# A layer step with a routed mixture of experts on one core: the first expert pair's tokens gathered by a product, late loads untied from the gather, the combine moved between two gates, the last down product in column halves

## The reference, cut to what matters

```python
def hier_moe(h, rg_w, rg_b, re_w, re_b, w_gate, w_up, w_down):
    ...
    lg = tf @ rg_w.astype(jnp.float32) + rg_b.astype(jnp.float32)
    grp = jnp.argmax(lg, axis=-1)
    ...
    top_v, top_i = lax.top_k(le, TOP_K_INNER)
    ...
    acc = jnp.zeros_like(t)
    for e in range(N_EXPERTS):
        hid = jax.nn.silu(t @ w_gate[e].astype(t.dtype)) * (t @ w_up[e].astype(t.dtype))
        acc = acc + combine[:, e:e + 1] * (hid @ w_down[e].astype(t.dtype))
    return acc.reshape(shp)
```

## Time and profile before

| | |
|---|---|
| median of 3 runs | 820.41 us (819.87 to 823.77) |
| the profiled execution's own time | 821.48 us |
| its span in the trace | 819.8 us |
| PE busy | 772.7 us (94%) |
| DVE, ACT, POOL busy | 270.4, 158.6, 139.1 us |
| mean rate of the DMA engines | 304 GB/s over the span |

### The profile page before, as it was taken

One profiled execution on the slowest core, in us unless ns is written; L12 is line 12 of the kernel. 1 busy time (PEld: TensorE's weight loads), 2 busy tenths in 40 slices (PEclk: granted clock), 3 DMA queues, 4 the chain that ended last, 5 costly groups with the idle time before them and its releaser, 6 DMA issues.

```text
span 819.8 us, 8712 instructions
## 1 busy us (share of the span) xinstructions
PE 772.7 (94%) x3488; PEld 372.7 (45%) x3488; DVE 270.4 (33%) x614; ACT 158.6 (19%) x313; POOL 139.1 (17%) x167
## 2 busy tenths in 40 slices
PE   4999999989999999889999999999998999899996
PEld 3777677758743334544333333333333333333332
DVE  2059999995355632521111101110110111011001
ACT  3211121234541101300211111111111111101114
POOL 2069899702002000010000000000000000000000
PEclk9999999999999999989999999999999999999999
DMA  9894200041508189989999999999999999999981
GB/s 275 301 350 166 103 20 0 2 110 41 167 26 265 57 276 348 419 320 427 426 426 426 427 429 424 427 429 425 426 426 428 426 426 427 427 428 426 429 335 65
DMA packets 51256, 249.58 MB, mean 304 GB/s; under 512 B 6966, under 2 KB 24406, under 8 KB 38655
## 3 DMA queue, kind: packets, MB, share of 16 engines
q1 hardware_dynamic: 45540, 243.54, 74.1%
q10 hardware_dynamic: 3147, 2.67, 1.1%
q0 software_dynamic: 2528, 2.79, 1.1%
HBM read 246.87 MB, written 8.61 MB: 312 GB/s over the span
## 4 chain that ended last, share of the span: by engine, by line
PE 71%; DVE 4%; issue 3%; ACT 2%; DMA 0%; DVEq 0%; ACTq 0%; POOLq 0%
PE bank L1177 27%; PE bank L1200 14%; PE bank L1051 9%; PE bank L1218 8%; PE bank L1160 2%; PE bank L1189 1%; PE bank L1024 1%; PE bank L1015 1%; DVE bank L1571 1%; PE bank L788 1%; PE bank L1178 1%; PE bank L1040 1%; PE bank L885 1%; DVE bank L1600 1%; DVE region_a L1570 1%
## 5 line engine op out<-in xcount | busy, mean ns | idle before, releaser
L788 PE MATMUL bank<-region_a,ring 128*128 128x320 f32 x576 | 158.7, 437 | 0.5 <-DVE region_a L1570 0.5
L1178 PE MATMUL bank<-ring,zz 128*64 128x512 f32 x304 | 135.3, 601 | 0.0
L788 PEld LDWEIGHTS bank<-region_a,ring 128*128 128x128 f32 x576 | 109.8, 192 | 46.5 <-issue 2.2
L1177 PE MATMUL bank<-ring,zz 128*64 128x512 f32 x272 | 122.9, 608 | 8.6 <-issue 8.0
L1570 DVE TENSOR_TENSOR region_a<-region_a,bank 64x512 f32<-64x512 f32 (+1 forms) x33 | 22.5, 680 | 328.6 <-ACT region_a L1497 328.4
L1571 DVE SCALAR_TENSOR_TENSOR bank<-region_a,par,bank 128x256 f32<-128x256 f32 x232 | 91.2, 483 | 0.0
L744 POOL DMA_INDIRECT region_a<-hn_scratch,region_a x16 | 15.9, 995 | 379.1 <-PE bank L1160 362.6
L1218 PE MATMUL bank<-zz,masks 128*128 128x512 f32 (+1 forms) x192 | 75.3, 609 | 2.1 <-ACT zz L1503 2.1
L1177 PEld LDWEIGHTS bank<-ring,zz 128*64 128x64 f32 x272 | 37.1, 140 | 83.7 <-issue 82.9
L1051 PE MATMUL bank<-ring,x_v_y 128*128 128x512 f32 (+1 forms) x192 | 74.1, 606 | 0.8 <-DVE x_v_y L1570 0.8
L1503 ACT ACTIVATE zz<-bank 64x512 f32<-64x512 f32 x64 | 37.8, 591 | 169.5 <-PE bank L1200 169.1
(11 more groups left out here) (310 smaller groups left out, 806.2 us busy)
## 6 DMA issues: line engine op xcount, KB each, us to landing
ring<-in_expert_w_up SPq DMA_DIRECT2D x19, 2048.0 KB, 33.7
ring<-in_expert_w_down SPq DMA_DIRECT2D x18, 2048.0 KB, 38.0
ring<-in_expert_w_gate SPq DMA_DIRECT2D x16, 2048.0 KB, 35.6
ring<-in_w_in SPq DMA_DIRECT2D x9, 2048.0 KB, 20.0
x_v_y<-in_expert_w_down SPq DMA_DIRECT2D x7, 2048.0 KB, 28.0
x_v_y<-in_expert_w_gate SPq DMA_DIRECT2D x5, 2048.0 KB, 42.5
ring<-in_w_out SPq DMA_DIRECT2D x4, 2048.0 KB, 9.1
xcx<-in_expert_w_gate SPq DMA_DIRECT2D x4, 2048.0 KB, 35.8
```

What stands on the lines that cost most here:

```text
L788: ins = pe.matmul(pt[0:m, 0:T], w[:, k, :], ht[:, k, :], start=k == 0, stop=k == KD - 1)
L1177: pe.matmul(to[0:CAP, :], x[:, k, :], wg[:, FE * k:FE * k + FE], **st)
L1178: ins = pe.matmul(to[CAP:P, :], x[:, k, :], wu[:, FE * k:FE * k + FE], **st)
```

## The change

It has four parts.

1. **First pair by a product.** Pair 0 isn't gathered. DVE builds `first`, a one-hot selection of tokens by slots for experts 0 and 1, scaled by 1/rms, and PE multiplies the raw rows in `xt` with it: `first_tokens(h)`, 12 products of 128 x 128, for each half. They stand around the `slots` product, and the `residual` products are spread: tile 1's first half goes ahead of `rank`, tile 2 behind it, tile 1's second half last. POOL gathers pairs 1 to 15.
2. **Late loads.** Load 8 waits for the router's last logits alone, load 9 for `hn_out`, load 10 still for `kept`.
3. **Combine between gates.** combine(i-2) stands between gate_up(2i) and gate_up(2i+1).
4. **The end.** The last down product is made in two column halves, in two banks; ACT copies the first half while PE makes the second; the last combine goes by column halves, with the 64-token tile last; the final norm follows that order, and the sample output's second half is stored from ACT's queue.

```diff
@@ SP
             sp_.wait_ge(filled, J[("lg2",)] + 1)
+            load_expert(n_slot - 3)
             sp_.wait_ge(S("hn_out"), 48)
-            load_expert(n_slot - 3)
-            sp_.wait_ge(S("gath"), 16)
             load_expert(n_slot - 2)
             sp_.wait_ge(S("kept"), 1)
             load_expert(n_slot - 1)
@@ PE
             residual(0)
+            residual(1, [0])
             pe.wait_ge(S("chosen"), 1)
...
             counts(ones, 2, 3, start=False, stop=True).then_inc(filled, 1)
+            residual(2)
...
+            def first_tokens(h):
+                to = job_bank("tokens", (0, h))
+                for k in range(4):
+                    for r, (t0, n) in enumerate(TILES):
+                        if h == 0 and k == 0:
+                            pe.wait_ge(S("first"), r + 1)
+                        ins = pe.matmul(to[:, P * k:P * k + P], xt[0:n, r, 4 * h + k:D:KD], first[0:n, r, :],
+                                        start=r == 0, stop=r == 2)
+                ins.then_inc(S("xg_T"), 1)
+                return ins
...
+            first_tokens(0)
             pe.wait_ge(S("osel"), 1)
-            slot_values(take(pe, "slots")).then_inc(filled, 1)
-            residual(1)
-            residual(2).then_inc(S("kept"), 1)
+            slot_values(take(pe, "slots"), osel).then_inc(filled, 1)
+            first_tokens(1)
+            residual(1, [1]).then_inc(S("kept"), 1)
...
+            def down_half(to, x, wd, q):
+                for k in range(4):
+                    for h in range(2):
+                        c0 = D * k + 512 * q + 256 * h
+                        ins = pe.matmul(to[CAP * h:CAP * h + CAP, 0:256], x[:, k, :], wd[:, c0:c0 + 256],
+                                        start=k == 0, stop=k == 3)
+                return ins
...
             for i in range(NE // 2):
                 for e in (2 * i, 2 * i + 1):
+                    if i >= 2 and e % 2:
+                        combine(i - 2)
                     gate, up = expert_landed(pe, 0, e), expert_landed(pe, 1, e)
...
                 if more:
-                    pe.wait_ge(S("gath"), 16 * (i + 2))
-                    tokens_T(i + 1, 0)
-                if i >= 2:
-                    combine(i - 2)
-                if more:
-                    tokens_T(i + 1, 1)
+                    pe.wait_ge(S("gath"), 16 * (i + 1))
+                    for h in range(2):
+                        tokens_T(i + 1, h)
...
             expert_down(NE - 2)
-            expert_down(NE - 1)
+            w_down = expert_landed(pe, 2, NE - 1)
+            down_half(job_free(pe, "down", NE - 1), hidt[:, :, own_half[1]], w_down, 0).then_inc(S("dn_half"), 1)
+            pe.wait_ge(S("hidt"), NE // 2)
+            down_half(job_bank("hidden", NE // 2 - 1), hidt[:, :, own_half[1]], w_down, 1).then_inc(S("dn_done"), 1)
...
+            pe.wait_ge(S("yo_half"), 1)
+            for r in range(2):
+                to_tile(back[1], yo_of, r, 0, end=True).then_inc(S("summed"), 1)
             pe.wait_ge(S("yo"), NE)
-            to_tokens(back[1], yo_of, end=True)
+            for r in range(2):
+                to_tile(back[1], yo_of, r, 1, end=True).then_inc(S("summed"), 1)
+            to_tile(back[1], yo_of, 2, 0, end=True)
+            to_tile(back[1], yo_of, 2, 1, end=True).then_inc(S("summed"), 1)
@@ DVE
+            link(dve.tensor_scalar(first_off, aa[:, :, 0:2], -BIG, BIG, ALU.mult, ALU.add))
...
             pt = got(dve, "rank")
-            link(tt_(tee, ee, bc(r3(pt[:, 0:3 * NE]).unsqueeze(1), [P, 2, 3, NE]), ALU.mult))
+            link(tt_(first_at, r3(pt[:, 0:3 * NE])[:, :, 0:2], first_off, ALU.add))
+            for r, (t0, n) in enumerate(TILES):
+                for j in range(2):
+                    ins = dve.tensor_scalar(first[0:n, r, CAP * j:CAP * j + CAP], slotno[0:n, :],
+                                            first_at[0:n, r, j:j + 1], rst[0:n, 3 + r:4 + r],
+                                            ALU.is_equal, ALU.mult)
+                ins.then_inc(S("first"), 1)
+            tt_(tee, ee, bc(r3(pt[:, 0:3 * NE]).unsqueeze(1), [P, 2, 3, NE]), ALU.mult).then_inc(S("tee"), 1)
+            dve.tensor_copy(cnt, pt[:, 3 * NE:4 * NE]).then_inc(free["dve"], 1)
```

More of the change, by code:

```diff
@@ L145, in bank_table @@
     until.update({name: len(JOBS) for name in OUT_JOBS})
-    banks, prev, last, held, own = [], [], {}, {}, {}
+    banks, prev, last, held, own = [], [], {}, {}, {("rank",): 2, ("slots",): 2}
     b = -1
@@ L328, in build @@
         val = moe(2 * 3 * 2 * NE).rearrange("p (o u c e) -> p o u c e", o=2, u=3, c=2)
-        osel = zf[:, 0:2 * 3 * CAP].rearrange("p (o u s) -> p o u s", o=2, u=3)
+        osel, osel_more = (zf[:, D * b:D * b + 2 * 3 * CAP].rearrange("p (o u s) -> p o u s", o=2, u=3) for b in (1, 0))
+        first = r3(zf[:, 2048:2048 + 3 * P])
+        first_off, first_at = (r3(zf[:, 2048 + 3 * P + 6 * b:2048 + 3 * P + 6 * b + 6]) for b in range(2))
         slotno = moe(CAP)
@@ L740, in carry_wait @@
                 pool.tensor_tensor(wait_word[:, w:w + 1], halfrow, halfrow, ALU.add)
-            for i in range(NE // 2):
-                wait(pool, S("xg_T"), 2 * i)
+            for i in range(1, NE // 2):
+                if i > 1:
+                    pool.wait_ge(S("xg_T"), 2 * i)
                 pool.indirect_dma_start(gat, None, hn_dram[:, :],
@@ L1110, in _, with residual @@
             logits(take(pe, "lg2"), 2).then_inc(filled, 1)
-            def residual(r):
+            def residual(r, halves=range(2)):
                 n = TILES[r][1]
                 pe.wait_ge(S("x2"), r + 1)
-                for q in range(2):
+                for q in halves:
                     dst = acc[2 * r + q][:, :] if r < 2 else acc[4][TS * q:TS * q + TS, :]
@@ L1136, in _, with slot_values @@
             counts(ones, 2, 3, start=False, stop=True).then_inc(filled, 1)
-            def slot_values(pt):
+            residual(2)
+            def slot_values(pt, osel):
                 for n_, (r, w) in enumerate([(r, w) for r in range(3) for w in range(2)]):
@@ L1207, in expert_down, with to_tile, to_tokens @@
                 down(job_free(pe, "down", e), hidt[:, :, own_half[e % 2]], w_down).then_inc(S("dn_done"), 1)
-            def to_tokens(rows, of, end=False):
-                k = rows.shape[0]
+            def to_tile(rows, of, r, q, end=False):
+                t0, n = TILES[r]
+                dst = acc[2 * r + q][:, :] if r < 2 else acc[4][TS * q:TS * q + TS, :]
+                return pe.matmul(dst, rows[:, t0:t0 + n], of[q][0:rows.shape[0], :], start=False, stop=end)
+            def to_tokens(rows, of):
                 for r in (2, 0, 1):
-                    t0, n = TILES[r]
                     for q in range(2):
[L1217 to L1220, removed]
+                        ins = to_tile(rows, of, r, q)
                 return ins
@@ L1518, in _, with half_back @@
             rows_back(NE - 2)
-            rows_back(NE - 1)
+            def half_back(pt, q):
+                for h in range(2):
+                    ins = act.activation(yo[own_half[1], 512 * q + 256 * h:512 * q + 256 * h + 256],
+                                         pt[CAP * h:CAP * h + CAP, 0:256], ACT.Copy)
+                return ins
+            act.wait_ge(S("dn_half"), 1)
+            half_back(job_bank("down", NE - 1), 0).then_inc(S("yo_half"), 1)
+            act.wait_ge(S("dn_done"), NE)
+            half_back(job_bank("hidden", NE // 2 - 1), 1).then_inc(S("yo"), 1)
             over = act.value_load(mcount[0:1, 0:1], min_val=0, max_val=T)
@@ L1914, in tokens_more @@
                            bc(lnffn[:, :].unsqueeze(2), [P, KD, CAP]), ALU.mult)
-            for h in range(2):
-                tokens(0, h)
+            tokens(0, 0)
+            pair_indices(got(dve, "slots")).then_inc(S("idx"), 1)
+            slot_indices(got(dve, "slots"))
+            pair_values(got(dve, "slots")).then_inc(free["dve"], 1)
+            tokens(0, 1)
             def places(b, tok, w):
@@ L1940, in _ @@
                     dve.wait_ge(S("sl_own"), q + 1)
[L1941 removed]
+                    slot_select(osel_more).then_inc(S("sl_osel"), 1)
                     dve.wait_ge(S("sl_slots"), q + 1)
```

57 lines of the change are left out of this document (28 added, 29 removed).

## The result

| | before | changed |
|---|---|---|
| median | 823.60 us (819.87 to 823.77, 5 runs) | 829.92 us (826.93 to 831.55, 5 runs) |
| profiled execution | 821.48 us, span 819.8 | 826.93 us, span 825.1 |

The ratio is 1.0083, with a 95% interval of 1.0061 to 1.0105. 814.0 was forecast with a range up to 818.2; the changed kernel lies above the range, on the side that had 4 in 100. The forecast stood on a median of 820.41 us for the kernel before; over all five runs it is 823.60, so 3.2 of the 15.9 us between forecast and measurement are the base. Put as a change, 6.4 us gained were forecast and 6.3 us lost were measured.

What follows compares the result with a forecast made beforehand. The weight stream was taken to bound the later pairs, 30.0 us per pair against PE's 27.3. Gains 4.1 + 3.1 - 1.0 + 0.2 = 6.4 us took 821.48 to 815.1, as median 814.0 us; range 811.8 to 818.2.

Steps and rivals of the forecast that it cites:

- Cost of `first_tokens`: Pair 0's product: each half's 12 products, two pass records each, were to take 2.75 us at full clock.
- The clock: PE's clock around the router and pair 0's product: expected at 1.00 from 348 us on.
- rival 1: Router stays at the lower clock: load 10 lands at 369.6, stream gains 1.6 us, time 816.5; chance 0.20.
- With the clock low throughout it would be 820: Router and pair 0's product: time in us if PE's clock never recovered there.
- Load 10: Weight stream after the router: kept at 358.1, issue at 358.6, landing near 367.1 us instead of 371.2.
- the stream gain of 4.1: Weight stream: load 10's earlier landing puts the stream 4.1 us ahead (3.4 to 4.9), and later loads keep it.
- PE gains 0.5 us: Router to first gate product: pair 0's products nearly use up the removed gather; start 358.2 instead of 358.67 us.
- This costs nothing else: Pair 0's selection: DVE's new work lies beside PE's, so there is no further cost.
- Part 3: Last pairs: combine between gates removes waits of 1.2 and 1.92 us, 3.1 us gained; PE's pair becomes 27.7 us.
- Clock drop at gate_up(30): Last pair: a wait of about 2.3 us may lower PE's clock, 1.0 us lost (0 to 1.9).
- Part 4: Kernel's end: halved last down product, hidden copy and reordered norm, 0.2 us gained (-0.3 to 0.8).
- Rival 3: PE's pair gets too long through waits ahead of down, making PE the bound; slower, about 826 us; chance 0.04.

Runs made afterwards that it cites:

- the first experiment: Changed kernel with `first_tokens` reading contiguous columns instead of every eighth, so pair 0's arithmetic is altered: 820.07 us, ratio 0.9997 to the kernel before.
- part 3 alone: Kernel before with only the combine moved between the two gates, pair 0 still gathered: 820.45 us, ratio 0.9963.
- experiment 3: Changed kernel with `first_tokens` reading contiguous columns, pair 0's arithmetic altered, run once more for its trace: 827.46 us.
- part 4 alone: Kernel before with only the new end, pair 0 still gathered: 823.85 us, ratio 1.0006.
- experiment 4: Changed kernel with the four column groups of each `first_tokens` read at steps 1, 2, 4 and 8, pair 0's tokens wrong: 828.55 us, one run.
- experiment 5: Changed kernel with pair 0's operands exchanged: `first` stationary, `xt` moving 512 columns, six products, then transposes: 819.86 us, ratio 0.9965.

## Why the prediction was wrong, by its steps

- **Cost of `first_tokens`: the step that failed.** "24 x 3.67 / 32 = 2.75 us at full clock". At full clock it is 4.4 us even with contiguous columns, and in the changed kernel it was 8.1. The row of the mixer has 16 products that each fill columns of their own; here three products in a row add into the same columns. In the timeline of the first experiment the weight loads of successive products start in pairs, and the pairs do not follow each other at the pace within one:

```profile
352.03 0.19 PEld L1159 LDWEIGHTS bank<-zz,x_v_y 128*128 128x128 f32 x1
352.30 0.19 PEld L1159 LDWEIGHTS bank<-zz,x_v_y 128*128 128x128 f32 x1
352.41 0.19 PEld L1159 LDWEIGHTS bank<-zz,x_v_y 128*128 128x128 f32 x1
```

  0.11 us within a product, as in the earlier trace rows, then 0.27 to the next. Whether the sum in the same columns causes it was not tried; 8.8 us for 48 records is measured. By this the two halves cost 3.3 us more than forecast at the upper clock.
- **The clock: the other half of the same step.** It was put at full with 0.20 for rival 1. In all five runs of the changed kernel the mean clock was 0.975 to 0.979, and in its trace the clock was 1.00 from 344.4 to 347.8 and 0.5 in every microsecond from 350 to 370, while PE is shown busy without a gap. That and the step of eight, which the forecast left out, make 16.2 us of 8.8, and slots takes 1.75 and the last residual 2.07 us, for which 1.3 and 0.9 were forecast. Rival 1 named the mechanism, but let the clock recover half way and priced the records at the mixer's pace: "With the clock low throughout it would be 820" was ten us short of the 829.9 measured. By its own rows it is rather 822: two times 5.5, slots 1.75 and a residual of 1.8 put kept at 365.8 and the landing at 374.8, 3.6 us behind the 371.2 of before instead of 4.1 ahead. The Trainium skill (page TensorE: Matmul & The Clock Gate, Part 1) has activity release the throttle, and I read that as a PE busy in the trace. That reading failed here: PE, busy in all 20 us from 350 to 370, stayed at 1.2 GHz. It did recover at 370, 2 us into gate_up(0).
- **Load 10.** Load 9 early and load 10 tied to `kept`: right. 7.7 to 9.2 us to landing: 7.8. Kept at 358.1: wrong by 10 us, all from the steps above, and with it the stream gain of 4.1, which became a loss.
- **"PE gains 0.5 us", "This costs nothing else".** Behind `rank` PE lost 11.3 us (22.9 for 11.65), which reach up(30) as 9.7.
- **Part 3: right in mechanism and size.** 3.1 forecast, 3.2 in the accounting of the spans, and 0.9963 for it alone, 3.0 us. Wait ahead of down 0.40: 0.41. Pair 27.7: 27.80. Waits ahead of gate_up(28) and (30) 1.2 and 2.3: 1.66 and 1.67.
- **Clock drop at gate_up(30), 1.0 lost: did not come.** Between 750 and 775 the clock was 1.00. The length of the wait does not settle it: behind waits of 2.72 us (part 3 alone, at 736.51) and 3.04 us (experiment 3, at 771.56) the clock stayed at 1.00 too, where before it fell behind 2.23.
- **Part 4: sign wrong, size small.** PE is done 3.55 us behind the start of the last down and combines at once, as forecast. From there to the end of the last scaling it is 13.1 us instead of 13.2, about the 0.2 gained that was forecast. What the forecast left out is the store: behind the last scaling (821.24 + 0.75) 3.1 us remain to the span's end, where before it was 2.5 (815.91 + 1.41 to 819.8). So 0.2 gained was 0.5 lost in this trace, and the interval of part 4 alone (0.9994 to 1.0018) holds both. The last store takes 2.7 us from ACT's queue to its landing, where the last one before took 2.0 from SP's. The two stores of the changed kernel, and the stores before:

```profile
out_y_sample<-x_v_y SPq DMA_DIRECT2D x1, 128.0 KB, 2.4
out_y_sample<-x_v_y ACTq DMA_DIRECT2D x1, 128.0 KB, 2.7
```

```profile
out_y_prompt<-x_v_y SPq DMA_DIRECT2D x4, 256.0 KB, 2.0
```

- **Rival 3, the slower one,** rested on PE's pair; that stayed at 27.80, and the kernel became slower for another reason, one that had its place among the rivals with the wrong price.

## What to carry to other kernels

Price a new product by a row that agrees with it in everything: moving columns, fresh weights per product, the step with which the weights are read, whether successive products add into the same columns, and the clock of that very stretch. Where the moving and the stationary operand can be exchanged, try the form with few weight loads and 512 moving columns: here it was the cheaper one, even with its transposes, and the only one whose mean clock stayed at 0.986 or above in every run. Freeing a transfer from a wait helps only as far as the slots of the next ones are freed earlier too, and a small urgent gather behind queued 2 MB loads pays for them: here it took 7.0 to 10.0 us instead of 3.2.

## What was not expected of the hardware

- The same instructions took 8.8 us or 14.6 us in two executions of one kernel, as the granted clock was 1.00 or 0.57, and 12 runs fell seven to five, with 5.5 us of free space between the groups. In the two traces the router's place differs too: in the faster execution `rank` starts at 348.80 behind a stretch at the low clock (0.50 from 342 to 346), in the slower one at 345.36, with the clock at 1.00 from 344 to 349, and it falls 1.1 us into `first_tokens(0)`. The place of `rank` doesn't settle it: in experiment 4 `rank` starts at 349.75, behind a low stretch as in the faster execution, the clock is 1.00 from 349 to 355, and it falls all the same in the first half's products. What lowers it stays open; the six long products of experiment 5 kept 1.00 in all 20 runs of the two kernels that have them, by their mean clocks of 0.986 to 0.992.
- A weight load of 128 x 128 floats took 186 ns at the upper clock and 333 at the lower (medians of `first_tokens`), with contiguous columns in both; with a step of eight four loads took 312 to 337 ns at the upper clock already.
